# A streaming encoder step on one core: second attention by pairs of heads, and side work laid out anew beside it

## The reference, cut to what matters

```python
proj = x @ w_in        # sb_q, sb_k, sb_v, c_q, c_kv, k_r, gate_a, gate_b
q    = rms_norm(c_q) @ w_uq;  ckv = rms_norm(c_kv);  kpe = rope(k_r)
o_a  = stick_breaking_attend(sb_q, k_sb, v_sb)          # 8 heads of 64
s    = (q_nope . (ckv @ w_uk) + q_pe . kpe) * 96 ** -0.5
o_b  = softmax(where(k_pos // 64 <= q_pos // 64, s, -inf)) @ (ckv @ w_uv)   # 8 heads
h    = layer_norm(ALPHA * x + (sigmoid(g_a) * (o_a @ w_oa) + sigmoid(g_b) * (o_b @ w_ob)) @ w_out)
# PEER: per token and head two top-16 lists of 128 sub-keys each, top 16 of the 256 sums
g    = softmax(top_s);  act = gelu(h . peer_u[experts])
y    = layer_norm(ALPHA * h + sum over 8 heads * 16 of (g * act) * peer_v[experts])
```

## Time and profile before

| | |
|---|---|
| median of 3 runs | 3556.41 us (3551.92 to 3557.34) |
| the profiled execution | 3558.26 us |
| its span in the trace | 3556.5 us |
| busy, share of the span | PE (TensorE) 85%, DVE (VectorE) 71%, ACT (ScalarE) 34%, POOL (GpSimd) 44% |
| mean granted TensorE clock | 0.914 |
| mean DMA rate | 309 GB/s |

### The profile page before, as it was taken

How to read it: one execution, slowest core, us unless ns; L and a number is a source line. 1 busy time by engine, 2 the same in 40 slices (tenths; PEclk the granted TensorE clock), 3 DMA queues, 4 the chain that set the end, 5 groups by cost and what they waited for, 6 DMA issues and landing times. The chain is left out here.

```text
span 3556.5 us, 36144 instructions
## 1 busy us (share of the span) xinstructions
...
## 2 busy tenths in 40 slices
...
GB/s 144 217 254 177 190 311 394 207 181 202 222 321 359 338 341 218 145 202 181 183 248 301 406 404 399 399 405 396 404 378 412 400 407 398 397 393 407 400 408 204
DMA packets 375912, 1098.51 MB, mean 309 GB/s; under 512 B 91712, under 2 KB 210208, under 8 KB 289568
## 3 DMA queue, kind: packets, MB, share of 16 engines
...
...
## 5 line engine op out<-in xcount | busy, mean ns | idle before, releaser
L428 POOL DMA_INDIRECT expert_rows<-in_experts,picked_index x640 | 770.9, 1204 | 1271.1 <-DVE ff_sum L583 1157.1
L571 DVE SCALAR_TENSOR_TENSOR expert_rows<-expert_rows,h_tile 128x1024 f32<-128x1024 f32 x672 | 820.1, 1220 | 256.8 <-DMA expert_rows<-in_experts,picked_index 212.4
L583 DVE SCALAR_TENSOR_TENSOR ff_sum<-expert_rows,coefficients,ff_sum 128x1024 f32<-128x1024 f32 x672 | 860.8, 1281 | 92.2 <-ACT coefficients L534 75.9
L1786 PE MATMUL dense_act_ps<-dense_hT,key_columns 128*128 128x384 f32 x2048 | 724.7, 510 | 139.5 <-DMA key_columns<-in_key_columns 128.5
L451 POOL DMA_INDIRECT gates_by_expert<-dense_gate,gate_address x384 | 680.3, 1772 | 154.7 <-issue 129.2
L1775 PE MATMUL dense_out_ps<-dense_value_rows,dense_weights 128*128 128x512 f32 x1536 | 678.9, 592 | 0.5 <-DVE dense_weights L1854 0.5
L1786 PEld LDWEIGHTS dense_act_ps<-dense_hT,key_columns 128*128 128x128 f32 x2048 | 399.4, 198 | 482.8 <-DMA key_columns<-in_key_columns 196.2
L833 PE MATMUL proj_ps<-xT,w_in_block 128*128 128x384 f32 (+1 forms) x1392 | 424.1, 468 | 40.7 <-PEq L1595 16.5
L1775 PEld LDWEIGHTS dense_out_ps<-dense_value_rows,dense_weights 128*128 128x128 f32 x1536 | 291.8, 190 | 342.6 <-issue 309.7
L833 PEld LDWEIGHTS proj_ps<-xT,w_in_block 128*128 128x128 f32 x1392 | 268.3, 193 | 195.7 <-issue 37.9
L528 ACT ACTIVATE activated<-dots 128x1 f32<-128x1 f32 (+1 forms) x631 | 124.8, 198 | 638.5 <-DVE expert_rows L571 601.5
...
...
## 6 DMA issues: line engine op xcount, KB each, us to landing
key_columns<-in_key_columns SPq DMA_DIRECT2D x128, 512.0 KB, 11.6
dense_value_rows<-in_experts SPq DMA_DIRECT2D x128, 512.0 KB
...
dense_gates<-gates_by_expert SPq DMA_DIRECT2D x128, 192.0 KB
...
```

What stands on the lines that cost most here:

```text
L428: pool.indirect_dma_start(to, None, self.a["experts"], bass.IndirectOffsetOnAxis(ap=index[:, k:k + 1], axis=0)).then_inc(self.got[p % self ...
L571: dve.scalar_tensor_tensor(place, place, 1.0, self.h[n % 2][:], ALU.mult, ALU.mult, accum_out=self.dots[:, s % TOPK:s % TOPK + 1]).then_in ...
L583: dve.scalar_tensor_tensor(total, self.ring[:, p % self.RING, D:2 * D], self.coef[:, y % TOPK:y % TOPK + 1], total, ALU.mult, ALU.add).the ...
L1786: mm = nc.tensor.matmul(up[it % 2][:, 0:W], keys[it % KB][:, k, :], hTd[:, k, :], start=(k == 0), stop=(k == KC - 1))
```

## The change

SHARES, the routing order and the second attention change; sums over groups 1 and 2 stay at 275 row steps and 48 heads. Scores of the second attention now are issued two heads ahead into three buffers of two banks; the turned probabilities have one bank, so that a tile with more than four key tiles is turned and copied in two parts; values are multiplied for two heads at a time, turned, so that head 2q lands in partitions 0 to 63 and head 2q+1 in 64 to 127 of a bank, already as `obT` wants it. The sign and scale of the scores go into the query gain, so that a minimum replaces maximum and negation. The inverse sums are applied in `merge_norm`: TensorE turns them, ScalarE copies them, eight small matmuls spread them over partitions, and VectorE multiplies `obT` by them. Semaphore numbers per stage grow from 32 to 40.

```diff
-        ((1, "project"), 42, 1, 9, 10), ((1, "stick"), 18, 2, 5, 38), ((1, "mla_project"), 6, 1, 1, 16), ((1, "mla"), 18, 2, 4, 34),
-        ((1, "merge"), 17, 1, 2, 26), ((1, "scores"), 27, 1, 3, 12),
-        ((2, "project"), 40, 1, 9, 44), ((2, "stick"), 26, 2, 6, 72), ((2, "mla_project"), 7, 1, 2, 26), ((2, "mla"), 25, 2, 5, 70),
-        ((2, "merge"), 20, 1, 2, 48), ((2, "scores"), 29, 1, 0, 40),
+        ((1, "project"), 31, 1, 13, 10), ((1, "stick"), 28, 3, 1, 38), ((1, "mla_project"), 8, 1, 1, 16), ((1, "mla"), 24, 3, 1, 34),
+        ((1, "merge"), 16, 1, 3, 26), ((1, "scores"), 19, 1, 5, 20),
+        ((2, "project"), 30, 1, 12, 50), ((2, "stick"), 36, 3, 3, 72), ((2, "mla_project"), 8, 1, 1, 26), ((2, "mla"), 33, 3, 3, 66),
+        ((2, "merge"), 17, 1, 4, 48), ((2, "scores"), 25, 1, 1, 40),
         ((3, "dense"), 1000, 1, 24, 16),
...
-        self.routes = [*ahead(0, 1), *heads(SAMPLE), *ahead(4, 2, 3), *heads(5), *heads(6), *heads(7)]
+        pairs = [[(t, h) for t in (2, 3)] for h in range(HEADS)]
+        mixed = [(4, 0), (4, 1), *pairs[0], *pairs[1], (4, 2), *pairs[2], *pairs[3], (4, 3), *pairs[4], *pairs[5], (4, 4), (4, 5), *pairs[6],
+                 (4, 6), *pairs[7], (4, 7)]
+        self.routes = [*ahead(0, 1), *heads(SAMPLE), *mixed, *heads(5), *heads(6), *heads(7)]
...
@@ mla_project, vector @@
+            nc.vector.tensor_scalar(gain[:, 0:QC], gain[:, 0:QC], -MLA_SCALE, None, ALU.mult).then_inc(gain_scaled, 1)
+            dve.wait_ge(gain_scaled, 1)
...
@@ mla_attend @@
+        pT = [mem.at(f"probsT{3 * g.n + i}", FG + 69632 + 4096 * i, [P, 1024]) for i in range(3)]
+        sp = [s.enter_context(nc.psum_tensor(f"score_ps{3 * g.n + i}", [P, 1024], F32)) for i in range(3)]
+        tp, op = banks(nc, s, f"mla_ps_turned{g.n}_", 2)
+        parts = lambda i: [keys_of(i)[2][c:c + 4] for c in range(0, len(keys_of(i)[2]), 4)]
+        copies_before = [sum(len(parts(i)) for i, _ in items[:n]) for n in range(N + 1)]
...
+            def scores(t):
+                i, h = items[t]
+                r = rows_of(i)
+                first, nk, _ = keys_of(i)
+                if t >= 3:
+                    pe.wait_ge(p_done, t - 2)
+                for c in range(0, nk, 512):
+                    w = min(512, nk - c)
+                    mm = nc.tensor.matmul(sp[t % 3][0:r, c:c + w], f["mqT"][0:MD, h, g.at[i]:g.at[i] + r],
+                                          f["mkT"][0:MD, h, first + c:first + c + w], start=True, stop=True)
+                mm.then_inc(s_done, 1)
+
+            scores(0)
+            scores(1)
+            for n in range(N + 1):
+                if n + 2 < N:
+                    scores(n + 2)
+                if n < N:
                     i, h = items[n]
                     r = rows_of(i)
                     pe.wait_ge(p_done, n + 1)
+                    for y, part in enumerate(parts(i)):
+                        if n or y:
+                            pe.wait_ge(t_copied, copies_before[n] + y)
+                        for x, (off, rows, vt) in enumerate(part):
+                            mm = nc.tensor.transpose(tp[0:rows, P * x:P * x + r], p[n % 2][0:r, off:off + rows], m["ident"][0:r, 0:r])
+                        mm.then_inc(t_done, 1)
+                k = n - 1
+                if k >= 0 and k % 2:
+                    i, h = items[k]
+                    r, tiles = rows_of(i), keys_of(i)[2]
+                    pe.wait_ge(t_copied, copies_before[k + 1])
+                    if h == 1 and turn(i) >= 1:
+                        pe.wait_ge(o_copied, turn(i))
                     for x, (off, rows, vt) in enumerate(tiles):
+                        for par in range(2):
+                            first = HD * (h - 1 + par)
+                            mm = nc.tensor.matmul(op[half[par], P * (h // 2):P * (h // 2) + r], f["mv"][0:rows, vt, first:first + HD],
+                                                  pT[(k - 1 + par) % 3][0:rows, P * x:P * x + r], start=(x == 0), stop=(x == len(tiles) - 1),
+                                                  skip_group_check=True)
                     mm.then_inc(av_done, 1)
 
         @block.scalar
         def _(act):
+            for t in range(N + 2):
                 if t < N:
                     i, h = items[t]
                     r = rows_of(i)
                     nk = keys_of(i)[1]
                     act.wait_ge(nm_done, t + 1)
                     if t >= 2:
+                        act.wait_ge(t_done, copies_before[t - 1])
                     bg.exp_ln(act)
+                    nc.scalar.activation(p[t % 2][0:r, 0:nk], sp[t % 3][0:r, 0:nk], ACT.Exp, bias=nm[0:r, t:t + 1],
+                                         scale=-1.0, accum_out=rs[0:r, t:t + 1]).then_inc(p_done, 1)
                 n = t - 1
+                if 0 <= n < N:
                     i, h = items[n]
                     r = rows_of(i)
+                    if n >= 3:
+                        act.wait_ge(av_done, (n - 3) // 2 + 1)
+                    for y, part in enumerate(parts(i)):
+                        act.wait_ge(t_done, copies_before[n] + y + 1)
+                        if i < TILES:
+                            nc.scalar.copy(pT[n % 3][:, 512 * y:512 * y + P * len(part)], tp[:, 0:P * len(part)]).then_inc(t_copied, 1)
+                        else:
+                            nc.scalar.copy(pT[n % 3][0:NEW, 0:r], tp[0:NEW, 0:r])
+                            for x in (1, 2):
+                                ins = nc.scalar.copy(pT[n % 3][:, P * x:P * x + r], tp[:, P * x:P * x + r])
+                                if x == 2:
+                                    ins.then_inc(t_copied, 1)
+                n = t - 2
+                if n >= 0 and items[n][1] == HEADS - 1:
+                    i = items[n][0]
+                    r = rows_of(i)
+                    act.wait_ge(av_done, (n + 1) // 2)
+                    nc.scalar.copy(f["obT"][:, :, g.at[i]:g.at[i] + r], op[:].rearrange("p (x q) -> p x q", x=4)[:, :, 0:r]).then_inc(o_copied, 1)
+                bg.act(min(1.0, t / N))
 
...
-                    nc.vector.reduce_max(mx[0:r, t:t + 1], sp[t % 2][0:r, 0:nk], AX).then_inc(max_done, 1)
-                    dve.wait_ge(max_done, t + 1)
-                    nc.vector.tensor_scalar(nm[0:r, t:t + 1], mx[0:r, t:t + 1], -MLA_SCALE, None, ALU.mult).then_inc(nm_done, 1)
+                    nc.vector.tensor_reduce(nm[0:r, t:t + 1], sp[t % 3][0:r, 0:nk], AX, ALU.min).then_inc(nm_done, 1)
...
-                    dve.wait_ge(av_done, n + 1)
-                    dve.wait_ge(inv_done, turn(i) + 1)
-                    nc.vector.tensor_tensor(on[turn(i) % 2][0:r, :].rearrange("p (h d) -> p h d", h=HEADS),
-                                            op[0:r, :].rearrange("p (h d) -> p h d", h=HEADS),
-                                            ri[0:r, at].unsqueeze(2).broadcast_to([r, HEADS, HD]), ALU.mult).then_inc(on_done, 1)
-                n = t - 3
-                if 0 <= n < N and items[n][1] == HEADS - 1:
-                    i = items[n][0]
-                    r = rows_of(i)
-                    dve.wait_ge(oT_done, turn(i) + 1)
-                    nc.vector.tensor_copy(f["obT"][:, :, g.at[i]:g.at[i] + r],
-                                          oT[:].rearrange("p (x q) -> p x q", x=4)[:, :, 0:r]).then_inc(oT_copied, 1)
...
@@ merge_norm @@
+            for n, t in enumerate(g.tiles):
+                r = rows_of(t)
+                mm = nc.tensor.transpose(ps[4][0:HEADS, g.at[t]:g.at[t] + r], ri[0:r, HEADS * n:HEADS * (n + 1)], m["ident"][0:r, 0:r])
+            mm.then_inc(ri_turned, 1)
...
+                    if j == 0 and i == 1:
+                        pe.wait_ge(ri_copied, 1)
+                        for q in range(4):
+                            for par in range(2):
+                                pick = m["ident"][0:HEADS, 2 * q + par:2 * q + par + 1].broadcast_to([HEADS, HD])
+                                mm = nc.tensor.matmul(ps[q][HD * par:HD * par + HD, 0:W], pick, riT[0:HEADS, :], start=True, stop=True, skip_group_check=True)
+                            mm.then_inc(spread, 1)
+                        pe.wait_ge(scaled, 4)
...
+            act.wait_ge(ri_turned, 1)
+            nc.scalar.copy(riT[0:HEADS, :], ps[4][0:HEADS, 0:W]).then_inc(ri_copied, 1)
...
+            for q in range(4):
+                dve.wait_ge(spread, q + 1)
+                nc.vector.tensor_tensor(f["obT"][:, q, :], f["obT"][:, q, :], ps[q][:, 0:W], ALU.mult).then_inc(scaled, 1)
```

96 lines of the change are left out of this document (17 added, 79 removed).

## The result

The changed kernel takes 3674.53 us (median of 4 runs, 3668.31 to 3688.29) beside 3556.88 for the kernel before in the same session (4 runs, 3551.92 to 3560.44): ratio 1.0337, 95% interval [1.0305, 1.0369]. It is slower by 118 us, where 3551 was forecast and 3596 was the upper end of the range. The profiled execution took 3676.7 us, its span is 3674.9 us.

The account below looks back on a forecast made before the run. VectorE and the waits in its order were taken to bound the kernel, POOL second and only in group 2. Group 0's -2, group 1's -30 and group 2's +26 us gave -6: 3551 us, range 3502 to 3596.

Parts of the forecast that it names:

- The step that failed: Group 2's second attention: VectorE's waits fall from 35 us to about 16, making the stage 26 us shorter.
- the failed step: Group 1's second attention: 22 us shorter, with POOL's 105 us of adds and fetches allowed in a 99 us stage.
- Rival B: Second attentions: one bank of turned probabilities makes TensorE and ScalarE wait, so no gain there; 3599 us, chance 0.17.
- POOL in group 2: POOL's adds, fetches and loads set group 2's projection (+44 us) and stick-breaking (+9 us).
- Group 1's projection: 11 rows fewer and 4 heads more on VectorE, less part of its waits: +8 us (3 to 11).
- Its stick-breaking: Group 1's stick-breaking: 10 rows more and 4 heads fewer, some softplus waiting: -9 us (-13 to -3).
- Scores of group 2: 4 rows fewer, one head more, fewer coefficient waits: -4 us (-10 to +3).
- group 1's scores: Most of VectorE's 30.6 us of coefficient waits go: -8 us (-18 to +2).
- the serial piece: Merges: turning, copying and spreading the inverse sums, then multiplying, adds 4 us (0 to 10).
- Rival A: Group 2's first three stages: POOL's excess does not reach the stage's end; 3490 us, chance 0.2.
- Rival C: Group 2's stick-breaking: half of 72 adds cost 2.46 us instead of 1.78 beside rows, +24 us; 3575 us, chance 0.08.
- Rival D: Whole schedule: if neither bound holds, only VectorE's saved 16 us of small work remain; 3540 us, chance 0.1.

Follow-up runs that it names:

- attention_only: The changed kernel's new second attention and merge with the old SHARES and routing order of the kernel before: 3547.01 us, ratio 0.9986 to the kernel before.
- schedule_only: The kernel before with the new SHARES and routing order, its attention and merge as they were: 3666.36 us, ratio 1.0315.
- copies_first_b: The changed kernel with ScalarE copying the previous head's turned probabilities before the next head's exponentials instead of after: 3661.35 us, ratio 1.0305.
- adds_later: The changed kernel with fewer adds planned in group 2's projection (56 for 81) and stick-breaking (58 for 72): 3625.11 us, ratio 1.0193.
- heads_out: Against `attention_only`, three heads of routing moved from beside group 1's second attention to its merge: 3544.25 us, ratio 0.9965.
- stick_two: The changed kernel with rows in batches of two instead of three beside both stick-breaking stages: 3678.31 us, ratio 1.0340.
- heads_in: Against `attention_only`, three heads moved from beside group 1's stick-breaking into its second attention: 3559.82 us, ratio 1.0015.

## Why the prediction was wrong

The total was forecast 6 us below the kernel before and came out 118 us above it. Of these 124 us the two second attentions are 101: 69 in group 2 and 32 in group 1.

**The step that failed** is the one that sized the second attentions. In group 2 it is "its 35 us of waits (174 less 139) fall to about 16, as scores lie two ahead and nothing of the outputs is waited for: -26". VectorE's work was right (128.8 us busy; the minima 26.2 us, as the maxima were the earlier trace rows). Its idle time rose to 88 us in place of 16. The step treated waits as something left over by a lack of buffers. They are made by the order on three engines, and rows in batches of three (some 7 us of VectorE between two minima) stretch every turn of it. Of the 69 us by which group 2's term was off, 26 are a saving that did not come with the old shares either (`attention_only`), 27 are what the schedule costs with the old attention (`schedule_only`), and 16 needed both parts.

In group 1 (-22, measured +9.6) the failed step is another: "POOL would allow this: 34 adds and 24 fetches are 105 us, of which 20 may hang over, in a stage of 99". POOL ran 39 adds and 27 fetches there, as some had hung over from the stage before, and lost 9.0 us at the boundaries between heads, which the count left out. Its rows came late, and VectorE waited 23.9 us for them. The sentence that POOL is a bound "only in group 2" did not hold once rows had been moved to stand beside group 1's attentions.

**Rival B** named the right mechanism, the one bank with its half turns, and the wrong condition. Its point was a wait of 1.6 us per half turn. Measured in the changed kernel's attention 2 are 94.4 us over 25 waits, 3.8 each, but it is not ScalarE's time that fills them, it is what stands ahead of the copy (`copies_first_b`). By itself the single bank costs 6.7 us (173.7 against 167.0). Its price of 48 us stopped at "no gain" and could not give the 53 us of real loss, and in group 1 a second bank changed nothing (130.8 us).

**POOL in group 2** was foretold rightly as the bound of two stages, and nearly in sum: +53 for projection and stick-breaking, +48.2 measured. The split was wrong (+44 and +9, measured +25.4 and +22.8), so part of the good sum is luck. The projection was to start at 1172 and last to 1428; it started at 1192.3 and ended at 1428.8, so that the same end stands in both is chance and its length was 236.5 us instead of 256. Its first add ran 59 us after its start, not 64, adds took 1.68 us, not 1.78, and 200 adds of 209 planned had run at its end, so the hang-over was again about 20 us. Stick-breaking was to be 9 longer and was 22.8 longer: in the forecast POOL's 204 us were set against 195 before and the difference taken, though the stage before took 190.6 with VectorE and POOL meeting; the measured 214 is POOL's own count with the hang-over. `adds_later` shows that POOL set both.

**Group 1's projection**, 11 rows for 4 heads, was +10.7 by VectorE's sum and +13.2 measured, outside the +3 to +11 given for it. The prediction took 8 for waits that did not go. **Its stick-breaking** was -9 and came out +3. VectorE's busy time fell (113.6 to 107.3), by 6.3 us and not by the 13.0 of the sum. A head was priced too high for a full stage: 9.1 us is its way from start to end with the pauses between its steps, while three heads fewer took 21.8 us from VectorE's busy time in `heads_out`, 7.3 each. VectorE's idle time, on the other side, grew by 9.1 us, and 7.6 us of waits for rows are new in it. From 673.7 us to the stage's end at 789.1 POOL has no gap but the 0.30 us before an instruction and 4.8 us at two boundaries between heads. The ten rows more are ten fetches more in its queue, which the forecast did not count in this stage. Batches are excluded by `stick_two`. In `heads_in`, with three heads fewer and the old rows, the stage gained 9.6 of 27 us; there VectorE waits for ScalarE's part of the stage's own work (17.2 us, before the change 5.5) and not for rows, so with fewer heads another floor stands near 119 us.

**Scores of group 2** were -4 and came out +6.7. VectorE's waits for coefficients there are 44.7 us (6 waits) where `attention_only`, with the old list, has 27.5, and `schedule_only` has the same stage (113.1 us), so it is the new list; why one head between 25 rows makes these waits longer was not tested. In group 1's scores they fell from 30.6 to 6.0 us, as foretold, and the stage lost 6.3 of the 8 us. **Merges**: the serial piece was put at 4 us (0 to 10). Without rows beside it, in group 0, it is 5.5, and the timeline shows each part: turning 0.73 us, spreading 4.10, first multiplication at 275.82, products at 279.21.

```profile
269.75 0.73 PE L1494 MATMUL out_ps<-identity,inverse_sum 128*8 128x128 f32 x3 [4.85 <-PEq L1237]
270.41 4.21 PE L1513 MATMUL merge_ps<-sb_outT,w_o 128*128 128x288 f32 x8
274.55 4.10 PE L1509 MATMUL out_ps<-inverse_sumT,identity 8*64 8x288 f32 x16
279.21 3.79 PE L1513 MATMUL merge_ps<-mla_outT,w_o 128*128 128x288 f32 x8 [0.56 <-DVE mla_outT L1571]
```

**Rival A** is excluded for group 2 (`adds_later`). **Rival C** asked for dearer adds beside more rows. In stick-breaking of group 2, with 36 rows instead of 26, an add took 1739 ns on the mean against 1780:

```profile
L455 POOL DMA_INDIRECT gates_by_expert<-dense_gate,gate_address x76 | 132.1, 1739 | 23.1 <-issue 22.8 <-DVE ff_sum L587 0.3
```

So the extra 24 us of C did not come, but its mechanism is there. In this stage of the changed kernel the 25 adds that started while VectorE was in a row's product or sum took 2.02 us on the mean, the other 51 took 1.60; before the change it was 23 adds at 2.08 and 48 at 1.64. The share of dear adds hardly grew (33% after 32%), so the mean stayed. C's 2.46 us for half of the adds was one instruction's time and not the mean. The Trainium skill's page "SBUF — State Buffer", section "Who interferes with whom", lists a contention between a VectorE instruction with two SBUF inputs and a GpSimd instruction that reads SBUF. The trace agrees with it, add by add, at some 0.4 us each; no run changed the overlap alone. **Rival D**, that the schedule hardly matters, is wrong: `schedule_only` costs 3.15%.
